# Moving six parameter loads from SP's program to ACT's at the start of a two-layer decoder trunk

## The chip, the core and the metric

The kernel runs on one core of a Trainium2 chip. A core has a matrix engine (PE), a vector engine (DVE), an activation engine (ACT), a general engine (POOL) and a synchronising engine (SP). Each runs its own list of instructions strictly in order, and they meet at semaphores. SP and ACT can also issue DMA transfers, each into a queue of its own; an issue is an instruction in the list like any other. The metric is the device time of one execution in microseconds (us).

## The reference

The input is 512 tokens of width 1024, with 16 learned tokens put ahead of them (528 in all), in float32. It runs through two layers.

```python
# layer 0
proj = h @ w_in_ab                    # columns: u | q k v
a_out = s5_mixer(u, ...)              # diagonal complex state space, 32 groups of 16 channels, 64 states
b_out = stick_breaking_attention(q, k, v)
mix = concat([a_out, b_out]) @ w_out_ab
# layer 1
mix = hgrn2_mixer(h @ w_in_c) @ w_out_c
# both
h = layer_norm(ALPHA * h + mix)
h = layer_norm(ALPHA * h + square(relu(h @ mlp_w_up + b_up)) @ mlp_w_down + b_down)
```

The change concerns four parameters of `s5_mixer`, and only how they are loaded:

```python
b_mat = lax.complex(b_re, b_im)                       # (32 groups, 64 states, 16 channels)
b_bar = ((lam_bar - 1.0) / lam)[:, :, None] * b_mat
bu = einsum('blgh,gph->blgp', uf, b_bar)
c_mat = lax.complex(c_re, c_im)                       # (32 groups, 16 channels, 64 states)
y = real(einsum('blgp,ghp->blgh', states, c_mat)) + d * uf
```

## The kernel before

The hidden state `h` is held transposed: 8 chunks (`kc`) of 128 features by 528 tokens. Matrix products are made from float32 values split in two parts, a rounded high part and the rest: `hh` and `hl` for the hidden state, `wh` and `wl` for the weights. A product takes three matmuls (L545, L547, L549).

Weights come in slots of 1 MB. For each slot SP issues a load into `raw` (two buffers, L379; the first two slots L390), ACT makes `wh` from it (`high`, L946), POOL makes `wl` (`low`, L437), and PE multiplies. SP issues the load of slot s+2 when POOL has made `wl` of slot s.

The order of work is written out by hand in one block per engine. At the start it is:

- SP issues the meta tokens, the first half of `x` (L395), weight slot 0, the second half of `x` (L397), weight slot 1, then the six loads of the change: `s5_b_re` and `s5_b_im` into `bb` (L400), `s5_c_re` and `s5_c_im` into `cn`, twice each (L403). Then the weight stream goes on. `bb` is read in runs of 16 floats (64 bytes), 2048 runs a load; `cn` in runs of 64 floats (256 bytes), 512 runs a load.
- ACT issues 13 loads of small rows of parameters (L965, L966, L977, L978). Then, for each chunk `kc`, it waits until DVE has copied the chunk to `h` and makes its high part `hh` (L985). After chunk 3 it makes `wh` of slot 0, after chunk 7 `wh` of slot 1.
- PE turns `x` chunk by chunk into PSUM (L679, L682). It may be at most two chunks ahead of DVE's copies. Then it turns the rows of parameters (L687, L688) and starts on the products `uqk`.
- DVE copies chunk kc out of PSUM to `h` (L1266, L1267), then makes `hl` of chunk kc-1 (L1278), for which it waits until ACT has made `hh` of that chunk.
- POOL makes constants, then waits for `wh` of slot 0.

Six semaphore increments of 16 on `bc_in` tell that `bb` and `cn` are loaded. DVE waits for them ahead of L1364, PE ahead of the transposes of `cn` (L696), which stand behind all of the `uqk` products.

Of the kernel before, what the change touches and what calls it, by code (L numbers as in the profile page):

```python
# [89 lines left out]
def trunk(nc, x, meta, w_in_ab, s5_lam_re, s5_lam_im, s5_log_dt, s5_b_re, s5_b_im, s5_c_re, s5_c_im,  # L90
          s5_d, s5_w_glu, s5_b_glu, w_out_ab, w_in_c, hgrn_gamma, hgrn_norm_g, w_out_c,
          ln_mix_g, ln_mix_b, mlp_w_up, mlp_b_up, mlp_w_down, mlp_b_down, ln_mlp_g, ln_mlp_b, out):
    with ExitStack() as ctx:
        def sb(name, shape, dt=F32, where=ctx):
            return where.enter_context(nc.sbuf_tensor(name, shape, dt))

        def sem(name):
            return ctx.enter_context(nc.semaphore(name))


        h = sb("h", [P, KC, L])
# [30 lines left out]
        bb = sb("bb", [P, 2, 16, 16], F32, m0a)  # L132
        cn = sb("cn", [P, 2, 4, 2, 64], F32, m0a)
# [99 lines left out]
        bc_in = sem("bc_in")  # L233
# [140 lines left out]
        @block.sync  # L374
        def _(sp_):
            def load(i, c, src, kcs=KC):

                sp_.wait_ge(w_lo, i * 2 + (c - 1))
                sp_.dma_start(raw[:, c % 2, :].rearrange("p (k n) -> p k n", k=kcs), src).then_inc(w_in[c % 2], 16)  # L379

            def stream(name, w, cols, kcs, col0=0, skip=0):
                s0, slots, _, _ = STAGES[name]
                wv = w.rearrange("(k p) n -> p k n", p=P)
                with sp_.Fori(0, (slots - skip) // 2) as i:
                    for j in range(2):
                        load(i, s0 + skip + j, wv[:, :, bass.ds(i * (2 * cols) + (col0 + (skip + j) * cols), cols)], kcs)


            def first_slot(n):
                sp_.dma_start(raw[:, n, :].rearrange("p (k n) -> p k n", k=KC),  # L390
                              w_in_ab[0].rearrange("(k p) n -> p k n", p=P)[:, :, n * 256:(n + 1) * 256]).then_inc(w_in[n], 16)

            xv = x[0].rearrange("(t p) d -> p t d", p=P)
            sp_.dma_start(meta_tok[:, :], meta).then_inc(x_in, 16)
            sp_.dma_start(x_tok[:, :, 0:D // 2], xv[:, :, 0:D // 2]).then_inc(x_in, 16)  # L395
            first_slot(0)
            sp_.dma_start(x_tok[:, :, D // 2:D], xv[:, :, D // 2:D]).then_inc(x_in_2, 16)  # L397
            first_slot(1)
            for ri, src in enumerate([s5_b_re, s5_b_im]):
                sp_.dma_start(bb[:, ri], src[0].rearrange("(a s) p h -> (s p) a h", s=2)).then_inc(bc_in, 16)  # L400
            for ri, src in enumerate([s5_c_re, s5_c_im]):
                for dup in range(2):
                    sp_.dma_start(cn[:, ri, :, dup, :],  # L403
                                  src[0].rearrange("(q g) h p -> (g h) q p", q=4)).then_inc(bc_in, 16)
            stream("uqk", w_in_ab[0], 256, KC, skip=2)
            stream("v", w_in_ab[0], 256, KC, col0=1536)
            s0 = STAGES["glu"][0]
            load(0, s0, s5_w_glu[0].rearrange("(k p) n -> p k n", p=P), 4)
            stream("out_ab", w_out_ab[0], 256, KC)

            def mlp(layer):
                for half in range(2):
                    stream(f"up{layer}{half}", mlp_w_up[layer], 256, KC, col0=2048 * half)
                    stream(f"down{layer}{half}", mlp_w_down[layer][2048 * half:2048 * (half + 1), :], P, 16)

            mlp(0)
            stream("i", w_in_c[0], 256, KC, col0=2 * D)
            stream("f", w_in_c[0], 256, KC, col0=D)
            stream("g", w_in_c[0], 256, KC, col0=3 * D)
            stream("q", w_in_c[0], 256, KC, col0=0)  # L420
            stream("out_c", w_out_c[0], 256, KC)
            mlp(1)

            ov = out[0].rearrange("(t p) d -> p t d", p=P)
            for half in range(2):
                cols = slice(512 * half, 512 * (half + 1))
                for t in (0, 2):
                    sp_.wait_ge(ot_copied, 4 * half + t + 2)
                    sp_.dma_start(ov[:, t:t + 2, cols], o_tok[:, t:t + 2, cols]).then_inc(out_sem, 16)
            sp_.wait_ge(out_sem, 16 * 4)  # L430
# [3 lines left out]
        def _(pool):  # L434
# [17 lines left out]
            def lows(name, pairs=None):  # L452
                s0, slots, _, _ = STAGES[name]
                with pool.Fori(0, pairs if pairs is not None else slots // 2) as i:
                    for j in range(2):
                        low(i * 2 + (s0 + 2 + j), (s0 + j) % 2)
# [79 lines left out]
        def _(pe):  # L536
# [304 lines left out]


            s0, _, t0, per = STAGES["glu"]
            slot_tiles(s0, s0 % 2, t0, t0, per, 4, 512, hh, hl, (y_ready, 0))
            run("out_ab", KC, 256, hh, hl, (mix_ready, 0), order=[4, 5, 6, 7, 0, 1, 2, 3])
# [91 lines left out]
        def _(act):  # L937
# [30 lines left out]
            for r0, r1, src in [  # L968
# [7 lines left out]
            ]:  # L976
                act.dma_start(lin_b[r0:r1, :], src).then_inc(rows_in, 16)  # L977
            act.dma_start(ldt[96:112, :], s5_log_dt[0].rearrange("(a s) -> a s", s=2)).then_inc(rows_in, 16)  # L978
            act.sem_inc(evac, 2)
            act.sem_inc(o_evac, FREE)  # L980

# [118 lines left out]
            def into_tmp(name, func, **kw):  # L1100

                first = used[0]
                _, slots, _, per = STAGES[name]
                used[0] += slots * per

                def empty(i, t, o, par):
                    act.wait_ge(tmp_free, i * (2 * per) + (first + t + 1))
                    more = {k: v(i, t) for k, v in kw.items()}
                    return act.activation(halves(tmp[:, par, :]), o, func, **more)  # L1109
                return empty  # L1110
# [670 lines left out]
```

## Time and profile before

| | |
|---|---|
| median of 3 runs | 1669.98 us (1669.7 to 1670.14) |
| the profiled execution, its own time | 1669.7 us |
| its span (first to last instruction) | 1668.0 us |
| PE busy | 1526.2 us (92%) |
| DVE, POOL, ACT busy | 758.5, 538.1, 525.4 us (45%, 32%, 32%) |
| mean granted PE clock | 0.938 |
| DMA: SP's queue (q1), ACT's queue (q10) | 106.77 MB, 0.11 MB |

A busy share is an average over many stages. The change lies in the first 20 us or so, and its worth is read there. In the timelines a line of engine SPq or ACTq is the issue of a DMA on SP or ACT: its duration is how long the issuing engine's list stood at it, not how long the transfer took.

### The profile page before, as it was taken

Reading aid. Unit: us, or ns where it says so; the run is one execution under the profiler, and the core shown is the slowest. Engines: PE = TensorE matmul, PEld = TensorE weight load, DVE = VectorE, ACT = ScalarE, POOL = GpSimd, SP = SyncE. Lnnn points to the kernel's source line nnn. Section 1 sums busy time; section 2 is a strip of 40 time slices with the busy share of each in tenths; the row PEclk is TensorE's granted clock in tenths of the full one; section 3 lists DMA queues with packets and bytes.
Section 4 is the critical chain, followed back from the end, with each engine's and each line's share of the span. In section 5 each row is a group of like instructions: output and inputs, shape, how many; then the busy total and the mean of one; then the engine's idle time right before and its main releaser. Section 6 shows DMA issues by size and latency. Waiting matters only on the chain.

```text
span 1668.0 us, 28242 instructions
## 1 busy us (share of the span) xinstructions
PE 1526.2 (92%) x11290; PEld 1432.0 (86%) x11290; DVE 758.5 (45%) x1171; ACT 525.4 (32%) x776; POOL 538.1 (32%) x195
## 2 busy tenths in 40 slices
PE   6976468988999999999999999899899999999997
PEld 6976344458999999999989999788799999999996
DVE  7976974443554102421240787466537420044114
ACT  3253325552432212222323732222134221222213
POOL 3424512213234434343313334200041443434430
PEclk9987867798999999999999999878799999999999
DMA  6311000001222332323302222100021233232311
GB/s 174 94 58 51 1 1 0 0 0 57 70 76 82 94 100 76 101 82 95 96 28 69 86 76 97 55 0 0 0 76 52 86 91 101 76 101 84 93 50 51
DMA packets 142009, 107.67 MB, mean 65 GB/s; under 512 B 8096, under 2 KB 139376, under 8 KB 141952
## 3 DMA queue, kind: packets, MB, share of 16 engines
q1 hardware_dynamic: 141552, 106.77, 21.1%
q8 instruction: 40, 0.66, 0.2%
q10 hardware_dynamic: 400, 0.11, 0.0%
q14 instruction: 17, 0.14, 0.0%
HBM read 104.77 MB, written 2.10 MB: 64 GB/s over the span
## 4 chain that ended last, share of the span: by engine, by line
PE 77%; DVE 15%; ACT 4%; issue 3%; DMA 0%; DVEq 0%; ACTq 0%; SPq 0%
PE pb L545 19%; PE pb L547 19%; PE pb L549 19%; PE pb L791 2%; PE pb L657 2%; PE pb L645 2%; PE pb L898 2%; DVE uqk L1444 2%; PE pb L613 2%; PE pb L614 2%; PE pb L615 2%; DVE sg L1683 1%; PE pb L810 1%; PE pb L780 1%; DVE h L1596 1%
## 5 line engine op out<-in xcount | busy, mean ns | idle before, releaser
L437 POOL TENSOR_TENSOR wl<-raw,wh 128x2048 fp32r<-128x2048 f32 x97 | 454.1, 4681 | 842.0 <-ACT wh L946 842.0
L545 PE MATMUL pb<-hh,wh 128*128 128x264 f32 x1824 | 372.2, 286 | 15.7 <-DVE hl L1555 7.0
L547 PE MATMUL pb<-hl,wh 128*128 128x264 f32 x1824 | 370.2, 285 | 0.0
L549 PE MATMUL pb<-hh,wl 128*128 128x264 f32 x1824 | 370.0, 285 | 0.0
L545 PEld LDWEIGHTS pb<-hh,wh 128*128 128x128 f32 x1824 | 283.5, 191 | 20.3 <-issue 8.3
L547 PEld LDWEIGHTS pb<-hl,wh 128*128 128x128 f32 x1824 | 283.5, 191 | 0.0
L549 PEld LDWEIGHTS pb<-hh,wl 128*128 128x128 f32 x1824 | 283.1, 190 | 0.0
L1569 DVE SCALAR_TENSOR_TENSOR h<-h,tmp 128x528 f32 x48 | 36.6, 763 | 396.1 <-ACT tmp L1109 396.1
L545 PE MATMUL pb<-hidh,wh 128*128 128x264 f32 x1024 | 208.8, 285 | 0.0
L547 PE MATMUL pb<-hidl,wh 128*128 128x264 f32 x1024 | 208.3, 285 | 0.0
L549 PE MATMUL pb<-hidh,wl 128*128 128x264 f32 x1024 | 207.0, 283 | 0.0
L946 ACT ACTIVATE wh<-raw 128x2048 fp32r<-128x2048 f32 x97 | 185.0, 1907 | 0.0
L549 PEld LDWEIGHTS pb<-hidh,wl 128*128 128x128 f32 x1024 | 159.4, 189 | 0.0
L547 PEld LDWEIGHTS pb<-hidl,wh 128*128 128x128 f32 x1024 | 159.1, 188 | 0.0
L545 PEld LDWEIGHTS pb<-hidh,wh 128*128 128x128 f32 x1024 | 158.2, 189 | 0.0
L1618 DVE TENSOR_TENSOR tmq<-tmp 128x528 f32<-128x528 f32 x64 | 63.9, 999 | 193.3 <-ACT tmp L1109 193.3
L1109 ACT ACTIVATE tmp<-pb,cols_a 128x528 f32<-128x528 f32 x64 | 44.7, 702 | 266.9 <-PE pb L549 251.1
L1109 ACT ACTIVATE tmp<-pb 128x528 f32<-128x528 f32 x48 | 29.3, 611 | 253.0 <-PE pb L549 243.2
L613 PE MATMUL pb<-wh,hh 128*128 128x256 f32 x224 | 65.0, 290 | 11.1 <-ACT v L1010 11.1
L645 PE MATMUL pb<-mean_w,ident 128*128 128x128 f32 x528 | 68.8, 291 | 0.0
L645 PEld LDWEIGHTS pb<-mean_w,ident 128*128 128x128 f32 x528 | 67.9, 209 | 0.3
L614 PE MATMUL pb<-wl,hh 128*128 128x256 f32 x224 | 64.5, 288 | 0.0
(342 smaller groups left out, 1899.4 us busy)
## 6 DMA issues: line engine op xcount, KB each, us to landing
raw<-in_mlp_w_up SPq DMA_DIRECT2D x32, 1024.0 KB, 5.4
raw<-in_mlp_w_down SPq DMA_DIRECT2D x32, 1024.0 KB, 6.1
raw<-in_w_in_c SPq DMA_DIRECT2D x16, 1024.0 KB, 5.4
raw<-in_w_in_ab SPq DMA_DIRECT2D x8, 1024.0 KB, 5.4
raw<-in_w_out_ab SPq DMA_DIRECT2D x4, 1024.0 KB, 5.1
raw<-in_w_out_c SPq DMA_DIRECT2D x4, 1024.0 KB, 5.2
x_tok<-in_x SPq DMA_DIRECT2D x2, 1024.0 KB, 8.3
out_h<-o_tok SPq DMA_DIRECT2D x4, 512.0 KB, 3.1
```

The lines of the kernel that those rows point to most:

```text
L437: pool.tensor_tensor(wl[:, par, :], raw[:, par, :], wh[:, par, :].bitcast(F32), ALU.subtract).then_inc(w_lo, 1)
L545: pe.matmul(o[:, b, :], lh, rh[:, kc, b * LH:(b + 1) * LH], start=first, stop=False)
L547: pe.matmul(o[:, b, :], lh, rl[:, kc, b * LH:(b + 1) * LH], start=False, stop=False)
L549: mm = pe.matmul(o[:, b, :], ll, rh[:, kc, b * LH:(b + 1) * LH], start=False, stop=last)
L613: pe.matmul(o, hh[:, kc, a:a + P], wh[:, par, w], start=kc == 0, stop=False)
L614: pe.matmul(o, hh[:, kc, a:a + P], wl[:, par, w], start=False, stop=False)
L615: mm = pe.matmul(o, hl[:, kc, a:a + P], wh[:, par, w], start=False, stop=kc == KC - 1)
L645: pe.matmul(pb[:, bank, 0:P], ident[:, :], mean_w[:, :], start=True, stop=True)
L946: act.activation(wh[:, c % 2, :], raw[:, c % 2, :], ACT.Copy).then_inc(w_hi, 1)
L1109: return act.activation(halves(tmp[:, par, :]), o, func, **more)
L1569: STT(hm, hm, scale, tmp[:, (t0 + t) % 2, :], ALU.mult, ALU.add).then_inc(tmp_free, 1)
L1618: me.step(TT(a, r, r, ALU.mult))
```

## The change

The six loads leave SP's list and are put into ACT's, behind the 13 loads of small rows and ahead of the first `hh`. What they load, where to, and the semaphore they increment stay. In the changed file the lines of the ACT block up to there stand 6 lower in number (L985 is L985 again, `high` is L940, `low` is L431, and SP's slot loads keep L379).

```diff
@@ block of SP, behind the load of slot 1
-            for ri, src in enumerate([s5_b_re, s5_b_im]):
-                sp_.dma_start(bb[:, ri], src[0].rearrange("(a s) p h -> (s p) a h", s=2)).then_inc(bc_in, 16)
-            for ri, src in enumerate([s5_c_re, s5_c_im]):
-                for dup in range(2):
-                    sp_.dma_start(cn[:, ri, :, dup, :],
-                                  src[0].rearrange("(q g) h p -> (g h) q p", q=4)).then_inc(bc_in, 16)
@@ block of ACT
             act.dma_start(ldt[96:112, :], s5_log_dt[0].rearrange("(a s) -> a s", s=2)).then_inc(rows_in, 16)
+            for ri, src in enumerate([s5_b_re, s5_b_im]):
+                act.dma_start(bb[:, ri], src[0].rearrange("(a s) p h -> (s p) a h", s=2)).then_inc(bc_in, 16)
+            for ri, src in enumerate([s5_c_re, s5_c_im]):
+                for dup in range(2):
+                    act.dma_start(cn[:, ri, :, dup, :],
+                                  src[0].rearrange("(q g) h p -> (g h) q p", q=4)).then_inc(bc_in, 16)
             act.sem_inc(evac, 2)
             act.sem_inc(o_evac, FREE)
```

On SP, at the start of the program, the six issues go from between slot 1 and the loop that loads the further slots:

```order
 L397 DMA x_tok<-in_x 128x4x512
 L390 DMA raw<-in_w_in_ab 128x8x256
-L400 DMA bb<-in_s_b_re 128x16x16
-L400 DMA bb<-in_s_b_im 128x16x16
-L403 DMA cn<-in_s_c_re 128x4x64 x2
-L403 DMA cn<-in_s_c_im 128x4x64 x2
 L384 UNCONDITIONAL_BRANCH
```

What SP does next is the wait of slot 2's load for POOL. On ACT, the same place before the change, from the last row loads to `wh` of slot 1:

```order
L977 DMA lin_b<-in_hgrn_norm_g 8x128
L978 DMA ldt<-in_s_log_dt 16x2
L985 ACTIVATE hh<-h 128x528 x4
L946 ACTIVATE wh<-raw 128x2048
L985 ACTIVATE hh<-h 128x528 x4
L946 ACTIVATE wh<-raw 128x2048
```

And on ACT after the change:

```order
L971 DMA lin_b<-in_hgrn_norm_g 8x128
L972 DMA ldt<-in_s_log_dt 16x2
L974 DMA bb<-in_s_b_re 128x16x16
L974 DMA bb<-in_s_b_im 128x16x16
L977 DMA cn<-in_s_c_re 128x4x64 x2
L977 DMA cn<-in_s_c_im 128x4x64 x2
L985 ACTIVATE hh<-h 128x528 x4
L940 ACTIVATE wh<-raw 128x2048
L985 ACTIVATE hh<-h 128x528 x4
```

The first `hh` now stands behind six more issues. Nothing else changes its place on any engine.

## Rows read from the trace of the kernel before

**Rows 1.** The page: the chain of work that ended last, its share of the span by engine.

```profile
PE 77%; DVE 15%; ACT 4%; issue 3%; DMA 0%; DVEq 0%; ACTq 0%; SPq 0%
```

**Rows 2.** Waits of PE, 0 to 140 us: line, what released it, us in total, times, longest.

```profile
PE pb L613 <- ACT v L1010: 10.7, 1, 10.7
PE pb L679 <- DMA x_tok<-in_x: 7.2, 1, 7.2
```

**Rows 3.** Timeline of ACT, 0 to 60 us: start, duration, engine, line, what.

```profile
6.94 0.32 ACTq L978 DMA_DIRECT2D ldt<-in_s_log_dt  x1
9.42 0.65 ACT L985 ACTIVATE hh<-h 128x528 fp32r<-128x528 f32 x1 [7.34 <-DVE h L1267]
...
13.20 0.64 ACT L985 ACTIVATE hh<-h 128x528 fp32r<-128x528 f32 x1 [0.66 <-DVE h L1267]
13.75 1.89 ACT L946 ACTIVATE wh<-raw 128x2048 fp32r<-128x2048 f32 x1
15.55 0.63 ACT L985 ACTIVATE hh<-h 128x528 fp32r<-128x528 f32 x1
```

**Rows 4.** Timeline of SP's DMA issues, 0 to 60 us.

```profile
1.27 0.41 SPq L395 DMA_DIRECT2D x_tok<-in_x  x1
...
2.91 2.10 SPq L390 DMA_DIRECT2D raw<-in_w_in_ab  x1
5.06 4.09 SPq L400 DMA_DIRECT2D bb<-in_s_b_re  x1
9.19 6.72 SPq L400 DMA_DIRECT2D bb<-in_s_b_im  x1
15.95 1.51 SPq L403 DMA_DIRECT2D cn<-in_s_c_re  x2
17.50 1.06 SPq L403 DMA_DIRECT2D cn<-in_s_c_im  x2
```

**Rows 5.** Timeline of all engines, 0 to 26 us.

```profile
10.49 0.70 DVE L1278 TENSOR_TENSOR hl<-h,hh 128x528 fp32r<-128x528 f32 x1
...
15.73 4.56 POOL L437 TENSOR_TENSOR wl<-raw,wh 128x2048 fp32r<-128x2048 f32 x1 [12.42 <-ACT wh L946]
...
16.52 4.34 DVE L1278 TENSOR_TENSOR hl<-h,hh 128x528 fp32r<-128x528 f32 x1
...
23.77 0.78 PE L545 MATMUL pb<-hh,wh 128*128 128x264 f32 x2
```

**Rows 6.** DMA queue of SP (q1): packets, MB, share; 0:5.01, 0:9.15, 0:15.91 us.

```profile
q1 hardware_dynamic: 361, 0.74, 48.8%
...
q1 hardware_dynamic: 1586, 2.17, 72.9%
...
q1 hardware_dynamic: 5011, 4.38, 89.5%
```

**Rows 7.** DMA queues of SP (q1) and ACT (q10); 7:9, 11:15, 15:16 us.

```profile
q1 hardware_dynamic: 614, 0.63, 100.9%
q10 hardware_dynamic: 150, 0.05, 10.7%
...
q1 hardware_dynamic: 1387, 1.40, 108.2%
...
q1 hardware_dynamic: 1761, 0.14, 145.8%
```

**Rows 8.** Tiles bb and cn, their first readers: duration min/median/max, first and last start.

```profile
L1364 DVE TENSOR_TENSOR vq<-bb,pt x1: 424/424/424, 47.7 to 47.7; 128x256 f32<-128x256 f32 x1
...
L696 PE MATMUL pb<-ident,cn x8: 272/272/273, 94.9 to 95.7; 128*128 128x128 f32 x8
```

**Rows 9.** Timeline of DVE, 84 to 145 us; in brackets idle before, and releaser.

```profile
137.63 1.29 DVE L339 TENSOR_TENSOR bt<-wb,group 128x512 f32<-128x512 f32 x2 [21.26 <-PE pb L615]
```

**Rows 10.** Chain in order of time, 0 to 140 us: start, us, what.

```profile
27.63 0.44 PE pb L549 x2
...
28.36 0.24 PE pb L547 x2
```

## The prediction

> **What bounds the kernel now.** I read four views in this order. The chain that ended last is PE for 77% of the span, with DMA and SP's queue at 0% [rows 1]. So the streamed loads bind nothing in the bulk of the program, and a change to loads can count only where PE is idle. Next, who made PE wait early on: in the first 140 us, 7.2 us for the first half of `x` and 10.7 us for ACT in the stage `v`; neither was a wait for `bb` or `cn` [rows 2]. From 23.77 us PE is in the products [rows 5] and stays there. The start is thus a ramp of about 24 us that stands as a whole ahead of a PE-bound program: whatever moves its end moves everything behind it. Third, the timelines of the ramp. Its loop goes PE (turn) -> DVE (copy to `h`) -> ACT (`hh`) -> DVE (`hl`) -> next chunk. ACT finishes issuing its row loads at 6.94 + 0.32 = 7.26 us and then has nothing until the first `hh` at 9.42 [rows 3]: 2.16 us of slack. Fourth, the cost of the six issues where they stand now: SP's list stands at them from 5.06 to 17.50 + 1.06 = 18.56, which is 13.5 us [rows 4]. It costs nothing there, since SP's next item is the load of slot 2, which waits for POOL's first `wl`, and that ends at 15.73 + 4.56 = 20.29 [rows 5].
>
> **What the change takes away.** SP gets 13.5 us of its list back and cannot use them: it would only wait longer for 20.29. Gain 0. The weight and `x` transfers were ahead of `bb` in the same queue, so they do not land earlier either. Gain 0. The data of `bb` are first read at 47.7 us and those of `cn` at 94.9 [rows 8]. In 15 to 16 us 1761 packets went through the queue [rows 7] and the six loads hold 2 x 2048 + 4 x 512 = 6144, so their transfer is over a few us after the weights, at about 20 us at the latest. Both readers keep over 25 us of cover. The DVE work behind `bb` ends 21.26 us before its next wait for PE [rows 9]. Cost 0.
>
> **What it adds.** Six issues ahead of ACT's first `hh`. Behind them on ACT are all eight `hh`, `wh` of slot 0, `wh` of slot 1. DVE waits for each `hh` to make `hl`, and its next copy stands behind that; PE may be only two chunks ahead of the copies; POOL waits for `wh`. So the whole ramp waits for the moment T at which ACT is through.
>
> From T to the end of the ramp: by T DVE has already copied chunks 0 and 1 (they need no `hh`), so `hl` of chunk 0 starts T + 0.75 (one `hh` of 0.65 and a hand-over of 0.1). In the trace it is 13.20 - 10.49 = 2.71 us from that `hl` to the `hh` of chunk 3 [rows 3, 5]. So `hh` of chunk 3 starts at about T + 3.4 instead of 13.20, a shift of T - 9.8. Everything behind keeps its distances: `wh` of slot 0 follows at once, the `hh` of chunk 4 comes behind it (15.55) [rows 3], POOL's `wl` starts, and the `hl` of chunk 4, begun at 16.52 while POOL runs, takes 4.34 us and ends 0.57 after POOL's [rows 5]. That stall moves along, since it hangs on the same ACT order. With S the time of the six issues, T = 7.26 + S, and the shift is S - 2.5.
>
> **How long is S?** The trace shows these loads only on SP, behind 4 MB of other loads, so I bound it.
> - Low end: issues that meet an unfilled queue. The last two `cn` issues took 1.06 together, 0.53 each [rows 4]. Six of them: S = 3.2, shift +0.7.
> - High end: as on SP, S = 13.5, shift +11.0. A reason speaks against it: those 13.5 us began at 5.06 and were a wait for the engines to drain, which end their work at the same time wherever it was issued; by that T is no later than 18.6, shift +8.8.
> - Issuing rate only: from the first half of `x` to the end of slot 1, SP issued 3072 runs in 1.27 to 5.01, 3.74 us [rows 4]; with the 16 runs of the meta tokens, and 16 packets more for each of the five issues' increments, I count 3168 packets, 1.18 ns each. 6144 + 96 packets: 7.4 us, shift +4.9.
> - Queue depth. What was issued but not moved when an issue ended: at 5.01, 3168 - 361 = 2807; at 9.15, 5232 - 1586 = 3646 [rows 6]. The next issue then stood for 6.72 us. At its end, at 15.91, 7296 - 5011 = 2285 were open, which looks like a limit near 3600 and about 1 us of lag. On ACT the six loads make 6240 packets, so the last issue needs 6240 - 3600, some 2600, to be moved first. SP's weights are still moving: 1387 packets in 11 to 15 us [rows 7]. How the engines share between the queues is seen from 7 to 9 us: ACT's little row loads were all issued by 7.26, yet 150 packets of theirs went by beside 614 of SP's [rows 7], so ACT's queue does not pass the other. If they alternate one for one from about 11.5, ACT's has moved 1200 when the weights end, near 15.5; the other 1400 go at 1761 per us, 0.8 us. T is 16.4, with the lag up to 17.4.
>
> I take the last, since `bb`'s second load alone stood 6.72 us once the queue was full: T = 16.8, S = 9.5, shift +7.0. The second half of `x` and slot 0 are delayed by less than 1 us by the small packets between theirs, and nobody waits for them, because ACT is late anyway: 0.
>
> By the Trainium skill (DMA: Bandwidth & Descriptors, section "Queues, rings and completion order") each DMA engine goes round-robin between the queues that have work, a packet of some 9 to 17 descriptors at a time. That fits the 150 beside 614: single-run row loads get a turn only between longer runs of SP's. With long runs of `bb` it would be turn for turn, as in my estimate. If small transfers were let past instead, S would fall to the 7.4 of the issuing rate, and the sum to +4.9.
>
> **Clock.** PE begins its products at the slow pace: a pair of matmuls takes 0.44 us at 27.63 and 0.24 from 28.36 on [rows 10], about 4.3 us after the products begin. PE idles through the ramp now and will idle more. I take 0 for it, with +-0.5 us for another phase.
>
> **Sum.** Profiled execution 1669.7 + 7.0 = 1676.7 us. The median of the three runs is 0.28 above that execution: **1677.0 us**, +0.42%.
>
> **The rivals.**
> - *Issues are cheap in ACT's own, nearly empty queue* (S about 3.2). For it: row loads took 0.32 at the end of ACT's list [rows 3], while SP stood still at its own. Against: they are 16 runs each, `bb` is 2048, and 0.53 belonged to 512 runs. Time 1670.7, not slower by what can be measured. It decides below S = 5.8. The Trainium skill (same page, section "Issuing engines are not separate DMA queues") says that issuing from several engines only saves the time to initiate, usually small relative to the transfer; here 4.09 and 6.72 us for 128 KB [rows 4] speak otherwise. By that rule it would be this rival.
> - *Only the issuing rate counts.* 1669.98 + 4.9 = 1674.9. For it: ACT's queue starts with few packets. Against: 6240 is far over 3600.
> - *As long as on SP.* 1681.0. For it: same loads, engines as busy. Against: the drain argument above.
> - *The other side: PE reaches its fast pace before the products.* The turning of `x` would come in a denser block just ahead of them if ACT is the only thing waited for; the 4.3 us at 0.44 instead of 0.24 per pair [rows 10] are worth 4.3 x (1 - 0.24/0.44) = 2.0 us. It wins only if S is under 4.5 (shift under 2.0): with S = 3.2 the time would be 1668.7. Against: the stall under POOL's `wl` splits the block in any case.
>
> **How the numbers follow.** A difference under 0.2% (3.3 us) is about what a measurement of this kernel can't tell from none. Forecast (S from 8.5 to 11.3, 1676.0 to 1678.8): 0.54. Issuing rate: 0.2. As on SP: 0.08. Cheap: 0.12, of these 0.02 with the early clock. The remaining 0.06 is spread between cheap and issuing rate, half of it under the threshold, half over. Slower by over 0.2%: 0.54 + 0.2 + 0.08 + 0.03 = 0.85. Within: 0.14. Faster by over 0.2%, which even the early clock does not reach: 0.01. The range of 1672 to 1681 leaves out the cheap case below and little above.
>
> **What would show it.** On ACT, six issue rows from about 7.3, the first one short, the second or the `cn` ones standing for several us, and the first `hh` directly behind, near 16.8. SP free at about 5 us, its load of slot 2 later than now by about 7. First products near 30.8, and from there every stage at the old length; `bb`'s reader near 55 with no wait for DMA. A first `hh` before 13 would refute the queue depth; a first `hh` on time would refute the mechanism; a delay of the ramp without a delay of the end would show slack further on that I did not see.

## The result, and the profile after

| | before | after |
|---|---|---|
| median | 1669.84 us (4 runs, 1668.38 to 1670.14) | 1679.53 us (4 runs, 1677.81 to 1679.95) |
| ratio | | 1.0056, 95% interval 1.0042 to 1.0070 |
| span of the profiled execution | 1668.0 us | 1677.4 us |
| first product of `uqk` on PE | 23.77 us [rows 5] | 33.22 us |

The kernel became 9.7 us slower; 1677.0 was forecast. The ratio takes in three more runs of the changed kernel (1677.6 to 1679.18 us); the medians of the table come from the four runs each that it names. The chain still is PE's nearly throughout, with 1% of it now in ACT's issues [rows 1]:

```profile
PE 76%; DVE 15%; ACT 4%; issue 3%; ACTq 1%; DVEq 0%
```

The waits of PE in the first 145 us, the two that matter here. The wait for ACT in stage `v` (10.7 us again, L607 now) and that for `x` are the old ones [rows 2]; between them a new one of 9.0 us has come, for DVE's copy of chunk 2, which stands behind an `hl` that waits for ACT:

```profile
PE pb L673 <- DVE h L1267: 9.0, 1, 9.0
PE pb L673 <- DMA x_tok<-in_x: 7.4, 1, 7.4
```

The timeline of ACT answers to [rows 3, 4]. The reader is to see where the six issues stand, that the first takes 0.45 us and the next two 4.7 each (12.67 is two issues, of 4.67 and 0.53), and that the first `hh` comes at 19.21 and not at 9.42. From there on the order and nearly the distances are the old ones: `wh` of slot 0 4.0 us behind the first `hh` (4.3 before), then the `hh` of chunk 4.

```profile
7.13 0.32 ACTq L972 DMA_DIRECT2D ldt<-in_s_log_dt  x1
7.48 0.45 ACTq L974 DMA_DIRECT2D bb<-in_s_b_re  x1
7.95 4.68 ACTq L974 DMA_DIRECT2D bb<-in_s_b_im  x1
12.67 5.23 ACTq L977 DMA_DIRECT2D cn<-in_s_c_re  x2
17.93 1.09 ACTq L977 DMA_DIRECT2D cn<-in_s_c_im  x2
19.21 1.18 ACT L985 ACTIVATE hh<-h 128x528 fp32r<-128x528 f32 x2 [17.12 <-issue]
...
23.22 1.90 ACT L940 ACTIVATE wh<-raw 128x2048 fp32r<-128x2048 f32 x1
25.03 1.16 ACT L985 ACTIVATE hh<-h 128x528 fp32r<-128x528 f32 x2
```

SP's issues: it is through at 2.92 + 2.33 = 5.25 us and then waits for POOL until 29.89, where in the kernel before it was waiting from 18.56 to 20.48.

```profile
2.92 2.33 SPq L390 DMA_DIRECT2D raw<-in_w_in_ab  x1
29.89 24.89 SPq L379 DMA_DIRECT2D raw<-in_w_in_ab  x3
```

All engines, answering to [rows 5]: the first `hl`, POOL's `wl` of slot 0, DVE's `hl` stalled under it, and the first product.

```profile
19.95 0.71 DVE L1278 TENSOR_TENSOR hl<-h,hh 128x528 fp32r<-128x528 f32 x1 [9.17 <-ACT hh L985]
...
25.21 4.50 POOL L431 TENSOR_TENSOR wl<-raw,wh 128x2048 fp32r<-128x2048 f32 x1 [21.90 <-ACT wh L940]
...
25.75 4.52 DVE L1278 TENSOR_TENSOR hl<-h,hh 128x528 fp32r<-128x528 f32 x1 [0.52 <-ACT hh L985]
...
33.22 0.78 PE L539 MATMUL pb<-hh,wh 128*128 128x264 f32 x2
```

The queues (q1 of SP, q10 of ACT) by packets: in 13 to 13.5, in 17.5 to 18, and ACT's from the start to 11.63, 16.34 and 17.34 us.

```profile
q1 hardware_dynamic: 141, 0.14, 98.8%
q10 hardware_dynamic: 139, 0.01, 23.3%
...
q10 hardware_dynamic: 243, 0.02, 67.1%
...
q10 hardware_dynamic: 402, 0.11, 4.9%
...
q10 hardware_dynamic: 2467, 0.24, 13.2%
...
q10 hardware_dynamic: 4078, 0.34, 21.3%
```

The first window shows the two queues packet for packet, 141 and 139. The others are used below. A count takes in the few packets that are under way at the window's edge, and "gone" below is this count. "Open" packets are those issued into a queue and not yet gone. The first reader of `bb` starts 9.4 us later (47.7 before [rows 8]) and waits for no transfer:

```profile
L1364 DVE TENSOR_TENSOR vq<-bb,pt x1: 426/426/426, 57.1 to 57.1; 128x256 f32<-128x256 f32 x1
```

### The profile page after: what moved, and what is told of

The parts are those of the page before. It is cut to its first block, busy times and chain, and to the rows that moved or that the text cites. A ratio compares the mean times of both kernels' runs of the same rounds, so it can differ in the third digit from the quotient of the medians.

```text
span 1677.4 us, 28242 instructions
## 1 busy us (share of the span) xinstructions
PE 1524.7 (91%) x11290; PEld 1429.4 (85%) x11290; DVE 758.7 (45%) x1171; ACT 525.3 (31%) x776; POOL 538.0 (32%) x195
## 4 chain that ended last, share of the span: by engine, by line
PE 76%; DVE 15%; ACT 4%; issue 3%; ACTq 1%; DVEq 0%
PE pb L539 19%; PE pb L541 19%; PE pb L543 19%; PE pb L785 2%; PE pb L651 2%; PE pb L892 2%; DVE uqk L1444 2%; PE pb L607 2%; PE pb L639 2%; PE pb L608 2%; PE pb L609 2%; DVE sg L1683 1%; PE pb L804 1%; PE pb L774 1%; DVE gs L1684 1%
## 5 line engine op out<-in xcount | busy, mean ns | idle before, releaser
L431 POOL TENSOR_TENSOR wl<-raw,wh 128x2048 fp32r<-128x2048 f32 x97 | 454.0, 4681 | 853.9 <-ACT wh L940 853.9
L539 PE MATMUL pb<-hh,wh 128*128 128x264 f32 x1824 | 371.1, 286 | 17.4 <-ACT tmp L1109 7.3
L940 ACT ACTIVATE wh<-raw 128x2048 fp32r<-128x2048 f32 x97 | 184.9, 1907 | 0.0
L607 PE MATMUL pb<-wh,hh 128*128 128x256 f32 x224 | 65.6, 293 | 11.1 <-ACT v L1010 11.1
```

The lines of the kernel that those rows point to most:

```text
L431: pool.tensor_tensor(wl[:, par, :], raw[:, par, :], wh[:, par, :].bitcast(F32), ALU.subtract).then_inc(w_lo, 1)
L539: pe.matmul(o[:, b, :], lh, rh[:, kc, b * LH:(b + 1) * LH], start=first, stop=False)
L607: pe.matmul(o, hh[:, kc, a:a + P], wh[:, par, w], start=kc == 0, stop=False)
L940: act.activation(wh[:, c % 2, :], raw[:, c % 2, :], ACT.Copy).then_inc(w_hi, 1)
```

## The experiments

The theory: all of the loss is the time at which ACT gets to its first `hh`; call it T. It is 0.2 us after ACT is through with its issues. The ramp then ends 14.0 us later (19.21 to 33.22), and the program follows unchanged. The rivals are the mixed traffic (small packets between `x` and the weights) and a worth of SP's freed list. A second question is what sets T. All starts of products are from the profiled executions; they have no spread like that of the times.

**Loads on ACT, where it waits anyway.**

```diff
             act.activation(pt[:, 0, :], cols_b[:, 96:112], ACT.Exp).then_inc(par_act, 1)
+            # the six loads here, and not ahead of the first hh
             act.wait_ge(par_dve, 2)
```

> The six loads are on ACT, but behind the Exp of L992, where ACT waited 4.6 us for DVE in the trace of before. Held-ACT theory: they hold nobody; first hh at 9.4, products begin at 23.8, time within 1 us of before (1669.8). The 13.5 us that SP gets back are worth nothing. Rival (small packets on ACT's queue or the freed queue of SP matter by themselves): it keeps the +9.4 us of the changed kernel, or gains over 2 us.

Measured: 1668.42 us beside 1669.64 for before in the same session (this base holds for e1 to e4), ratio 0.9993 (0.9984 to 1.0002). ACT:

```profile
8.88 0.64 ACT L979 ACTIVATE hh<-h 128x528 fp32r<-128x528 f32 x1 [6.79 <-DVE h L1267]
...
23.01 1.89 ACT L940 ACTIVATE wh<-raw 128x2048 fp32r<-128x2048 f32 x1
24.46 0.40 ACTq L988 DMA_DIRECT2D bb<-in_s_b_re  x1
...
24.90 0.96 ACTq L988 DMA_DIRECT2D bb<-in_s_b_im  x1
25.89 1.78 ACTq L991 DMA_DIRECT2D cn<-in_s_c_re  x2
27.70 1.08 ACTq L991 DMA_DIRECT2D cn<-in_s_c_im  x2
```

The same six loads take 0.40, 0.96, 1.78 and 1.08 us here, 4.3 in all from 24.46 to 28.78, in a time in which ACT would wait for DVE anyway. The products begin at

```profile
23.36 0.78 PE L539 MATMUL pb<-hh,wh 128*128 128x264 f32 x2
```

That is 0.4 us earlier than before, as the first `hh` is 0.5 earlier. In time a difference from before can't be told: the interval goes from 2.7 us faster to 0.3 slower. So six issues on ACT's queue cost nothing measurable where ACT waits anyway, and a worth of SP's 13.5 us does not show.

**Only `bb`, and only `cn`, on ACT.**

```diff
 # e2: behind ldt on ACT, cn stays on SP
+            for ri, src in enumerate([s5_b_re, s5_b_im]):
+                act.dma_start(bb[:, ri], ...).then_inc(bc_in, 16)
 # e3: behind ldt on ACT, bb stays on SP
+            for ri, src in enumerate([s5_c_re, s5_c_im]):
+                for dup in range(2):
+                    act.dma_start(cn[:, ri, :, dup, :], ...).then_inc(bc_in, 16)
```

> Only the two bb loads go to ACT at the changed place, cn stays on SP. In the trace of the changed kernel the second bb issue ended at 12.63. Held-ACT theory: first hh at 12.8, products begin at 12.8 + 14.0 = 26.8, time +3.0 us (1672.8). Rival (the traffic of the 4096 runs of bb between x and the weights costs): bb makes two thirds of the packets, so two thirds of 9.4, +6.3 us.

> Only the four cn loads go to ACT. Four issues at 0.53 from 7.5: ACT is free at 9.6, first hh at 9.7, products begin at 23.8 to 24.0, time +0.2 us at most. By the traffic rival a third of 9.4, +3 us.

Measured with `bb`: 1671.69 us, ratio 1.0012 (1.0003 to 1.0021), and the second `bb` issue, the first two `hh` and the first product are

```profile
7.84 4.67 ACTq L978 DMA_DIRECT2D bb<-in_s_b_im  x1
...
12.71 1.18 ACT L985 ACTIVATE hh<-h 128x528 fp32r<-128x528 f32 x2 [10.62 <-issue]
...
26.72 0.78 PE L543 MATMUL pb<-hh,wh 128*128 128x264 f32 x2
```

The products begin at 26.72 for 26.8 expected. In time that is +2.1 us for +3.0, not +6.3 (the last section shows where about 1 us of such a difference comes from): `bb`'s packets go between the weights here as in the changed kernel, so the traffic rival falls. With `cn`: 1670.65 us (+1.0), ratio 1.0010 (1.0001 to 1.0019):

```profile
7.39 1.00 ACTq L977 DMA_DIRECT2D cn<-in_s_c_re  x2
...
8.42 2.26 ACTq L977 DMA_DIRECT2D cn<-in_s_c_im  x2
...
10.87 1.18 ACT L985 ACTIVATE hh<-h 128x528 fp32r<-128x528 f32 x2 [8.79 <-DVE h L1267]
...
24.89 0.78 PE L541 MATMUL pb<-hh,wh 128*128 128x264 f32 x2
```

This missed: the fourth `cn` issue took 1.70 us, not 0.53, so T is 10.87 for 9.7 and the products begin 1.1 us later than before. Again they are 14.0 behind T.

**ACT held without moving a load.** Nothing in the queues changes; ACT waits ahead of the first `hh`.

```diff
             act.dma_start(ldt[96:112, :], ...).then_inc(rows_in, 16)
+            act.wait_ge(bc_in, 16 * 6)      # e4
+            act.wait_ge(w_in[1], 16)        # e5, instead
```

> All loads stay on SP as in before; ACT waits ahead of the first hh until the last of the six has landed (issued 18.1, landing 3.2 us later: 21.3). No traffic is changed. Held-ACT theory: first hh at 21.3, products begin at 35.3, time +11.5 us. Traffic rival: no change.

> As before, but ACT waits ahead of the first hh until weight slot 1 has landed (16.5 in the trace of before). Held-ACT theory: first hh at 16.6, products begin at 30.6, time +6.8 us: what the prediction took for the changed kernel. A second point for the slope of one beside the hold until cn.

Measured, e4: 1680.84 us (+11.2 for +11.5), ratio 1.0069 (1.0054 to 1.0085).

```profile
21.21 1.18 ACT L986 ACTIVATE hh<-h 128x528 fp32r<-128x528 f32 x2 [19.12 <-DMA cn<-in_s_c_im]
...
35.22 0.78 PE L545 MATMUL pb<-hh,wh 128*128 128x264 f32 x2
```

e5: 1676.57 us beside 1669.2 for before (the base of e5 to e8; +7.4 for +6.8), ratio 1.0042 (1.0027 to 1.0057).

```profile
16.67 1.18 ACT L986 ACTIVATE hh<-h 128x528 fp32r<-128x528 f32 x2 [14.58 <-DMA raw<-in_w_in_ab]
...
30.69 0.78 PE L545 MATMUL pb<-hh,wh 128*128 128x264 f32 x2
```

35.22 for 35.3 and 30.69 for 30.6. Holding ACT is enough to make the loss, with the traffic of before. Over the changed kernel and e2 to e7, with T from 10.87 to 21.21, the first product came 14.01 or 14.02 us after T.

**What sets T: order and size of the loads.**

```diff
 # e6: the changed kernel, cn ahead of bb
 # e7: the changed kernel, each bb load in four
+                for a0 in range(0, 16, 4):
+                    act.dma_start(bb[:, ri, a0:a0 + 4, :],
+                                  src[0].rearrange("(a s) p h -> (s p) a h", s=2)[:, a0:a0 + 4, :]).then_inc(bc_in, 16)
 # and the two waits for bc_in at 16 * 12
```

> The changed kernel with the cn loads ahead of the bb loads on ACT. Theory W (an issue that does not fit into about 4100 to 4600 open packets waits until a whole earlier load has been retired, about 1 us after its last packet): the second bb issue waits for the four cn, 2512 packets of ACT's queue, gone at 16.4: ACT free at 17.5, products begin at 31.5, 1.7 us less than the changed kernel. Theory L (a blocked issue waits until the queue is nearly empty, about 1100 packets open as at 17.34): needs the first bb load gone too, 17.4 and later plus 1: ACT free at 18.4.

> The changed kernel with each bb load cut in four loads of 512 runs, so that all twelve loads are of 528 packets. Theory W: space comes back in pieces of 528; the eighth load goes at about 14.6, the four cn at 16.3, 17.1, 17.4, 17.7: ACT free at 18.3, products begin at 32.3, 0.9 us less than the changed kernel. Theory L (waits until nearly empty): blocked at the eighth until about 17, then five issues of 0.53: ACT free at 19.9, products at 33.9.

Measured, e6: 1677.26 us, ratio 1.0044 (1.0029 to 1.0059).

```profile
10.75 2.22 ACTq L978 DMA_DIRECT2D bb<-in_s_b_re  x1
13.00 4.96 ACTq L978 DMA_DIRECT2D bb<-in_s_b_im  x1
18.15 1.18 ACT L985 ACTIVATE hh<-h 128x528 fp32r<-128x528 f32 x2 [16.06 <-issue]
```

e7: 1678.28 us, ratio 1.0049 (1.0034 to 1.0064).

```profile
7.31 2.95 ACTq L975 DMA_DIRECT2D bb<-in_s_b_re  x4
10.29 6.37 ACTq L975 DMA_DIRECT2D bb<-in_s_b_im  x4
16.68 1.09 ACTq L979 DMA_DIRECT2D cn<-in_s_c_re  x2
...
19.08 1.18 ACT L987 ACTIVATE hh<-h 128x528 fp32r<-128x528 f32 x2 [17.00 <-issue]
```

ACT is free at 17.96 and 18.89 (T is 18.15 and 19.08): each lies between the two theories (17.5 and 18.4; 18.3 and 19.9). What tells them apart is not T but the single issues. In e7 the sixth quarter was let in at 14.41, and ACT's queue had moved, one microsecond earlier and then:

```profile
q10 hardware_dynamic: 916, 0.14, 6.8%
...
q10 hardware_dynamic: 1193, 0.16, 8.0%
```

With 2375 packets still open, that is far from an empty queue: theory L falls. Theory W's rule fits this issue: its row loads (400) and the first quarter (528) are 928 packets, and 916 had gone at 13.41. It also fits the changed kernel. The second `bb` issue ended at 12.63, when at 11.63 402 packets had gone (all 400 of the row loads, and the first two of `bb`); the first `cn` issue ended at 17.34, when at 16.34 2467 had gone, and row loads and first `bb` are 2464. In e2 the count 1 us ahead of the second issue's end was 408. W's size fails, though: I had put the limit between 4100 and 4600 packets, after the pair of `bb`, and in e3, e6 and e7 the fourth load of 528 stood for 1.35 to 1.70 us with about 2200 open at its end.

The rule of W fails as well, by rows that no run was made for. A `bb` load is 2064 packets, so in these rows "a whole earlier load has gone" and "some 2050 packets of the same queue are open ahead of this issue" are the same moment: 2464 - 402 = 2062, 4528 - 2467 = 2061, and 3040 - 916 = 2124 in e7. The two part where no load's end is near. In e2 SP's first `cn` issue, 528 packets alone, stood 4.01 us and ended at 9.15; one microsecond earlier 1253 packets of SP's queue had gone. SP's loads end at 560 and at 1600 packets, so none had just gone, but 3168 - 1253 = 1915 were open ahead.

```profile
L401 SPq DMA_DIRECT2D cn<-in_s_c_re x2: 1749/2879/4009, 5.1 to 9.2; - x2
...
q1 hardware_dynamic: 1253, 1.82, 72.4%
```

SP's first `bb` issue in the kernel before is a second such row: it ended at 9.15 too, with 1586 gone where slot 0 ends at 1600 [rows 6]. Over the ten traces 40 issues stood for more than 0.7 us, and in 34 of them 1890 to 2300 packets of the same queue were open ahead of the issue one microsecond before it ended. So the count of open packets ahead carries further than W. It is a reading of these traces and was not tried by a run of its own, and it leaves six out: the three fourth loads just named, with under 1750 open ahead from their start on, and three `cn` issues behind `bb` (in e1, e4 and e8), with 2590 to 3400 ahead. One of these is e1's first `cn` issue, which ended at 27.11: 4528 - 1132 = 3396 were open ahead at 26.11 and 1457 at its end. The microsecond is thus no fixed time either.

```profile
q10 hardware_dynamic: 1132, 0.15, 3.5%
...
q10 hardware_dynamic: 3071, 0.28, 8.0%
```

**Slot 0 first.** A try at a better ramp, on top of e1.

```diff
+            first_slot(0)
             sp_.dma_start(x_tok[:, :, 0:D // 2], xv[:, :, 0:D // 2]).then_inc(x_in, 16)
-            first_slot(0)
@@ ACT
+            high(0, 0)
             for kc in range(KC):
                 act.wait_ge(xt_res, 2 * (kc + 1))
                 act.activation(hh[:, kc, 0:L], h[:, kc, :], ACT.Copy).then_inc(xt_hi, 1)
-                if kc == 3:
-                    high(0, 0)
```

> Six loads on ACT behind the Exp of L992, weight slot 0 ahead of the first half of x on SP, and wh of slot 0 ahead of the first hh. wh at 7.1 to 9.0, POOL's wl 9.0 to 13.6, out of the way before DVE's hl of chunk 0 (about 13.7); x arrives 3.2 us later, the stall of 3.7 us under POOL and the wait of 0.8 for the second half of x go. Products begin at 22.4 instead of 23.8: 1.4 us faster, 1668.4, too little for the times to tell, the profile shows it.

Measured: 1668.58 us (12 runs), ratio 0.9999 (0.9989 to 1.0009).

```profile
7.51 1.91 ACT L940 ACTIVATE wh<-raw 128x2048 fp32r<-128x2048 f32 x1 [5.42 <-DMA raw<-in_w_in_ab]
...
22.72 0.78 PE L539 MATMUL pb<-hh,wh 128*128 128x264 f32 x2
```

The eight `hh` now come 1.2 to 1.55 us apart (12.56 to 21.79) with no stall under POOL's `wl`, and the products begin at 22.72, 1.05 us earlier than before and not 1.4. Of that 0.4 us was e1's already. It is seen in the profile and can't be told in the times.

## Why the prediction was right, and which term was off

- *SP gains nothing, readers keep their cover.* Right: e1, and the reader of `bb` above.
- *The ramp is shifted by T - 9.8.* Right: 19.21 - 9.8 = 9.4, and the first product moved by 33.22 - 23.77 = 9.45. The span grew by 9.4.
- *Small packets alternate with the weights one for one.* Right, 141 beside 139 (q1 and q10 above). It is the row on which the Trainium skill's round-robin (DMA: Bandwidth & Descriptors, "Queues, rings and completion order") bears, and the trace agrees with it.
- *The time of the six issues, S.* This is the term that was mis-sized: 9.5 us forecast, 19.01 - 7.45 = 11.6 measured. T is 19.2 for 16.8: 2.1 us of this is S, the rest a start 0.2 later and the step to the first `hh`. With these 2.4 us the sum is 1679.4 for 1679.53 measured. The step that failed is the one on the queue's depth, "so the last issue needs 6240 - 3600, some 2600, to be moved first". It read the limit as 3600 with the issue's own packets counted in, so that 2600 moved would do for the last issue. In truth already the first `cn` issue, the third of six, was held until 17.34, when 4078 - 400 = 3678 of their packets had gone; and the last three then took 0.53 each, one by one, 1.7 us together, which the sum had at nothing. That 17.34 lies at the upper end of the forecast's own 16.4 to 17.4 for T is in part luck, since it is the end of another issue. The 2285 open packets at the end of SP's second `bb` issue, which I called a lag, show the same as ACT's issues: at 14.91, 1 us before that issue's end, 3199 had gone, so 5232 - 3199 = 2033 were open ahead of it.
- *T no later than 18.6, since the engines end their work at the same time.* Wrong by 0.6. The premise nearly held: the last packet of the six loads went at 20.94 us, and at 20.59 in the kernel before. But when the issues end does not follow from it. While the `cn` issue was held, only the last weights and `bb` were there to move; in 17.5 to 18, just after it was let in, 243 packets went (above), a rate of 486 a microsecond where 1761 had been seen [rows 7]. The kernel before has such a gap too (145 packets in 16 to 16.5), so what the 0.6 us are made of, beyond the 0.2 of the step to the first `hh`, stays open.
- *The clock term, 0 with +-0.5 us.* The 0 came true by luck. The slow stretch is 4.30 us long in before and after alike, but the time behind the first product moved by -1.5 us in e5 and by +1.3 in e6, as the last section shows. The early fast clock did not come.
- *Rivals.* Cheap issues: the first took 0.45, like a row load, but only the first. Only the issuing rate: 7.4 us for 11.6, and the 1.18 ns a packet were not a rate of issuing alone, since slot 1's issue stood 2.10 us [rows 4] where slot 0's 1024 runs took 0.50. As long as on SP: 1681.0 came nearer to the time than my forecast, by the wrong reason. The measured 1679.53 lies between this and the band of 1676.0 to 1678.8 which had the chance of 0.54, and inside the range of 1672 to 1681.

## What to carry to other kernels

A DMA issue is an instruction of its engine, and its price is not that of a free queue: with more than some 2000 packets of its own queue open ahead of it, it stood, in most rows of this case, until enough of them had gone. How long that takes hangs on how fast the queue moves, and so on what the other queue is moving at the time. Put loads with many short runs where the issuing engine waits anyway and late in its list, not ahead of the first link of a chain; an engine that is seen to stand for 13 us at issues may be the one on which they are free. Ask of the engine that gets them what stands behind them.

## What was not expected of the hardware

The same six loads took 11.5 us to issue at 7.5 us and 4.3 at 24.5, on the same engine (the changed kernel and e1). In both the second `bb` issue ended with over 3700 packets open. What differs is how fast they went: in 12 to 15 us of the changed kernel ACT's queue moved 805 packets beside 804 of SP's, in 26 to 27 us of e1, with SP's queue empty, 1950.

The stretch in which PE runs its products at the slow pace (0.44 us a pair) had different lengths from kernel to kernel: 4.30 us in before and after, but 2.54 in e5 (30.69 to 33.23) and 5.61 in e6 (32.16 to 37.77), by the first piece of the chain that is faster. For e5 and e6:

```profile
33.23 0.40 PE pb L549 x2
```

```profile
37.77 0.28 PE pb L539 x2
```

The span behind the first product goes with it: 1642.7 us in e5, 1644.2 in before and after, 1645.5 in e6, and, ties aside, the ten kernels stand in the same order by both. So times that differ by some 3 us may differ by this alone, and e5's span grew by 5.4 us while its products began 6.9 later. Yet the pace explains only half: a slow stretch 1.8 us shorter saves 1.8 x (1 - 0.24/0.44) = 0.8 of the 1.5 us of e5, an estimate; the rest comes further on and was not traced. The two paces stand to each other like the clock's two levels, 1.2 and 2.4 GHz, though the granted clock of before shows 1.00 from 23 to 30 us. Why the length differs was not tried. The Trainium skill (TensorE: Matmul & The Clock Gate, "Part 1: The HAM clock gate") says that the point of the change shifts with where the first matmul falls, by half a microsecond either way; 2.54 to 5.61 is more than that. That is from ten programs with ten starts, one profile each.
